# Gate columns of the memory branch projected among the memory attention's rounds, in a fused three-layer model kernel

## What is computed

```python
h = _rms(x, attn_norm_g)
mem_n = _rms(mem, mem_norm_g)                       # 256 memory rows
mk = _rms(_heads(mem_n @ w_kv[:, :MEM_W], 4), mem_k_norm_g)
mv = _heads(mem_n @ w_kv[:, MEM_W:], 4)
mq = _rms(_heads(proj("mem_q"), 4), mem_q_norm_g)   # proj(name) = h @ its columns of w_in
y_mem = _merge_heads(_mem_attention(mq, mk, mv))    # 4 heads of width 256
y_fox = ...   # attention with a forget gate: 16 heads, q and k normed per head
branches = jnp.stack([y_fox, y_lru, y_sb, y_mem], axis=2)
gates = jax.nn.sigmoid(proj("gates").reshape(b, s, 4, 1024) + b_gate)
mixed = jnp.sum(gates * jnp.einsum('bsnc,ncd->bsnd', branches, w_branch), axis=2)
x = x + mixed @ w_out
```

## Time and profile before

| what | value |
|---|---|
| runs, us | 4116.31 (median), 4113.97, 4118.38 |
| profiled execution, us | 4122.55, its span 4120.8 |
| TensorE busy | 3855.2 us, 94% of the span |
| VectorE, ScalarE, GpSimd busy | 1940.8, 1490.6, 381.7 us |
| memory attention's rounds | from 2573.8 to 2664.7 us of the span |
| memory branch | from 2664.7 to 2751.9 us |

### The profile page before, as it was taken

How to read it: one execution, slowest core, us unless ns; L and a number is a source line. 1 busy time by engine, 2 the same in 40 slices (tenths; PEclk the granted TensorE clock), 3 DMA queues, 4 the chain that set the end, 5 groups by cost and what they waited for, 6 DMA issues and landing times.

```text
span 4120.8 us, 48423 instructions
## 1 busy us (share of the span) xinstructions
PE 3855.2 (94%) x17196; PEld 3050.2 (74%) x17196; DVE 1940.8 (47%) x3222; ACT 1490.6 (36%) x2451; POOL 381.7 (9%) x332
## 2 busy tenths in 40 slices
PE   8999997799999999987899998899999999899999
PEld 6887664588888887665688886777777768677877
DVE  4433467654334423567554344335544444645652
ACT  3222343432223223333432234436535553533221
POOL 0100001101001101011011021101000000100110
PEclk9999998899999999987899999999999989999999
DMA  4333221033333333211133333131122113223332
GB/s 119 96 97 108 69 59 47 10 100 97 97 91 92 97 97 109 59 44 34 40 94 95 106 114 91 40 87 44 47 72 62 47 43 93 74 82 87 97 92 97
DMA packets 484448, 321.89 MB, mean 78 GB/s; under 512 B 10928, under 2 KB 464176, under 8 KB 483280
## 3 DMA queue, kind: packets, MB, share of 16 engines
q1 hardware_dynamic: 479616, 301.81, 25.2%
q0 software_dynamic: 3536, 16.13, 1.2%
q10 hardware_dynamic: 1152, 2.10, 0.1%
HBM read 310.82 MB, written 8.52 MB: 77 GB/s over the span
## 4 chain that ended last, share of the span: by engine, by line
PE 73%; DVE 8%; ACT 7%; issue 6%; DVEq 4%; POOLq 0%; DMA 0%; ACTq 0%; POOL 0%; SPq 0%
PE bank L234 21%; PE bank L236 20%; PE bank L235 20%; ACT w_hi L219 2%; DVE w_lo L226 1%; PE bank L1188 1%; PE bank L2152 1%; DVEq L2455 1%; PE bank L1199 1%; PE bank L1191 1%; PE bank L1190 1%; PE bank L1172 1%; PE bank L974 1%; DVEq L2469 1%; DVEq L1013 1%
## 5 line engine op out<-in xcount | busy, mean ns | idle before, releaser
L234 PE MATMUL bank<-h_hi,w_hi 128*128 128x512 f32 x3064 | 1230.0, 401 | 68.3 <-DVE h_lo L386 24.9
L226 DVE TENSOR_TENSOR w_lo<-w_raw,w_hi 128x1024 fp32r<-128x1024 f32 (+1 forms) x571 | 742.4, 1301 | 1070.8 <-ACT w_hi L219 1067.5
L236 PE MATMUL bank<-h_lo,w_hi 128*128 128x512 f32 x3128 | 1230.1, 393 | 0.0
L235 PE MATMUL bank<-h_hi,w_lo 128*128 128x512 f32 x3064 | 1204.7, 393 | 0.0
L219 ACT ACTIVATE w_hi<-w_raw 128x1024 fp32r<-128x1024 f32 (+1 forms) x571 | 591.5, 1038 | 620.0 <-DMA w_raw<-in_ffn_w_down 316.6
L234 PEld LDWEIGHTS bank<-h_hi,w_hi 128*128 128x128 f32 x3064 | 579.6, 189 | 236.8 <-issue 101.4
L236 PEld LDWEIGHTS bank<-h_lo,w_hi 128*128 128x128 f32 x3128 | 591.4, 189 | 131.3 <-issue 2.3
L235 PEld LDWEIGHTS bank<-h_hi,w_lo 128*128 128x128 f32 x3064 | 579.3, 189 | 114.5 <-issue 2.0
L234 PE MATMUL bank<-g_hi,w_hi 128*128 (+1 forms) x880 | 343.7, 391 | 3.7 <-DVE gu_ring L2471 3.7
L235 PE MATMUL bank<-g_hi,w_lo 128*128 (+1 forms) x880 | 343.4, 390 | 0.0
L236 PE MATMUL bank<-g_lo,w_hi 128*128 (+1 forms) x880 | 343.3, 390 | 0.0
(11 more groups left out here) (438 smaller groups left out, 4628.7 us busy)
## 6 DMA issues: line engine op xcount, KB each, us to landing
w_raw<-in_w_in SPq DMA_DIRECT2D x105, 512.0 KB, 3.8
w_raw<-in_ffn_w_gate SPq DMA_DIRECT2D x88, 512.0 KB, 3.8
w_raw<-in_ffn_w_up SPq DMA_DIRECT2D x88, 512.0 KB, 3.8
w_raw<-in_ffn_w_down SPq DMA_DIRECT2D x88, 512.0 KB, 3.5
w_raw<-in_w_mix SPq DMA_DIRECT2D x50, 512.0 KB, 3.9
w_raw<-in_w_up SPq DMA_DIRECT2D x44, 512.0 KB, 3.8
w_raw<-in_w_branch SPq DMA_DIRECT2D x32, 512.0 KB, 3.7
w_raw<-in_w_down SPq DMA_DIRECT2D x22, 512.0 KB, 3.2
```

The lines of the kernel that those rows point to most:

```text
L226: dve.tensor_tensor(WL[:, slot(c), 0:w], RAW[:, slot(c), 0:w], WH[:, slot(c), 0:w].bitcast(F32), ALU.subtract).then_inc(w_lo, 1)
L234: pe.matmul(bank, wh, xh, start=start, stop=False)
L235: pe.matmul(bank, wl, xh, start=False, stop=False)
L236: return pe.matmul(bank, wh, xl, start=False, stop=stop)
```

## The change

The eight gate units of the memory branch leave the branch and follow the six units of the first two head pairs, as eight `copy` items; the list of items laid among the memory attention's rounds grows from 6 to 14, and the parts on TensorE from 24 to 48, on ScalarE and VectorE from 8 to 16. Their raw sums are copied to the tiles of `X`. The branch becomes eight units of `w_branch`, written out instead of looped, over banks 0 to 3 in turn; ScalarE takes Sigmoid from the tiles of `X` into the same ring of two. Ahead of the first of these units TensorE waits for the low parts of all heads. Nothing else is moved; the number of units, matmuls and loads is what it was.

```diff
-U_BR["mem"] = _u; _u += 16
+U_GATES["mem"] = _u; _u += KT
+U_BR["mem"] = _u; _u += KT
...
+    def gate_items(name, unit0, dst, free):
+        out_ = [item(U_GATES[name] - unit0 + u, "copy", dst(u)) for u in range(KT)]
+        for u, x in enumerate(out_):
+            x["free"] = free(u)
+        return out_
...
-    PF1, PS1 = PF + 6, PF + 30
+    PF1, PS1 = PF + 14, PF + 38
...
+    fox_items0 += gate_items("mem", U_FOX0, lambda u: X[:, u, :], lambda u: (x_parked, LAYERS * 16 + 16))
...
+    def stored_branch_sp(sp, c, n):
+        for u in range(KT):
+            load_cols(sp, 0, c + u, A["w_branch_2"][n], u * P)
+
+    def stored_branch_act(act, c, b, n, gate):
+        act.preload_act_table(ACT.Sigmoid)
+        act.drain()
+        for u in range(KT):
+            hi(act, 0, c + u + AHEAD)
+            act.wait_ge(mx_done, b * KT + u + 1)
+            act.activation(SG[:, u % 2, :], gate(u), ACT.Sigmoid, bias=v2(W_BG + n * KT + u)).then_inc(sg_done, 1)
+
+    def stored_branch_dve(dve, c, b):
+        dve.drain()
+        for u in range(KT):
+            m = b * KT + u
+            lo(dve, 0, c + u + AHEAD)
+            dve.wait_ge(w_used, c + u + 5)
+            dve.wait_ge(sg_done, m + 3)
+            if b == 0:
+                dve.tensor_tensor(MIXED[:, u, :], SG[:, u % 2, :], B[u % 4][:, :], ALU.mult).then_inc(mx_done, 1)
...
+    def stored_branch_pe(pe, c, b, ready, bank_read):
+        bank_read(pe)
+        ready(pe)
+        for u in range(KT):
+            split_ready(pe, 0, c + u)
+            if u >= 4:
+                pe.wait_ge(mx_done, b * KT + (u - 4) + 3)
+            for k in range(KT):
+                last = products(pe, B[u % 4][:, :], c + u, slice(k * P, (k + 1) * P), YH[:, k, :], YL[:, k, :],
+                                k == 0, k == KT - 1)
+            last.then_inc(w_used, 1)
...
         pairs(U_FOX0, (FOXQ, FOXK, FOXV), 0, 2)
-        branch_sp(sp, C0 + U_BR["mem"], BRANCH["mem"])
+        for u in range(KT):
+            load_cols(sp, 0, C0 + U_GATES["mem"] + u, A["w_in_2"], GATE + BRANCH["mem"] * D + u * P)
+        stored_branch_sp(sp, C0 + U_BR["mem"], BRANCH["mem"])
...
-        branch_act(act, C0 + U_BR["mem"], 0, BRANCH["mem"])
+        stored_branch_act(act, C0 + U_BR["mem"], 0, BRANCH["mem"], lambda u: X[:, u, :])
...
-        branch_dve(dve, C0 + U_BR["mem"], 0, BRANCH["mem"])
+        stored_branch_dve(dve, C0 + U_BR["mem"], 0)
...
-        branch_pe(pe, C0 + U_BR["mem"], 0, lambda e: e.wait_ge(y_lo, YF + 2),
+        stored_branch_pe(pe, C0 + U_BR["mem"], 0, lambda e: e.wait_ge(y_lo, YF + 2),
                   lambda e: e.wait_ge(pt_done, SM + 16 + 2))
```

More of the change, by code:

```diff
@@ L70 @@
 U_MEMQ = U_FOXF + 1
-U_BR = {}
+U_BR, U_GATES = {}, {}
 _u = U_MEMQ + 8
 U_FOX0 = _u; _u += 6
-U_BR["mem"] = _u; _u += 16
+U_GATES["mem"] = _u; _u += KT
+U_BR["mem"] = _u; _u += KT
 U_FOX = _u; _u += 18
@@ L2068, in branch_dve @@
         dve.drain()
+    def stored_branch_sp(sp, c, n):
[17 more added lines that the diff above has]
+                dve.tensor_tensor(MIXED[:, u, :], SG[:, u % 2, :], B[u % 4][:, :], ALU.mult).then_inc(mx_done, 1)
+            else:
+                dve.tensor_tensor(GU[:, u % 2, :], SG[:, u % 2, :], B[u % 4][:, :], ALU.mult).then_inc(mx_done, 1)
+                dve.drain()
+                dve.tensor_tensor(MIXED[:, u, :], MIXED[:, u, :], GU[:, u % 2, :], ALU.add)
+        dve.drain()
+    def stored_branch_pe(pe, c, b, ready, bank_read):
[9 more added lines that the diff above has]
+            last.then_inc(w_used, 1)
     def branch_pe(pe, c, b, ready, bank_read):
```

## The result

| | kernel before | changed kernel |
|---|---|---|
| runs, us, median (lowest to highest), 14 each | 4113.85 (4106.36 to 4124.28) | 4125.22 (4120.69 to 4134.23) |
| ratio to before, 95% interval | | 1.003 [1.0022, 1.0038] |
| profiled execution, us, and its span | 4122.55, 4120.8 | 4128.55, 4126.6 |
| changed stretch, us | 183.69 | 190.43 |

The change makes the kernel 0.3% slower. The changed stretch is measured between two instructions that both kernels have: TensorE's first matmul of the woven units (2570.30 before, 2568.81 after, each behind the same wait of 1.50 us) and its first scores of the forgetting attention (2753.99 before, 2759.24 after). The lines of the file move by one: L234 of before is L235 of after, L1310 is L1311, L1362 is L1363.

A forecast was written before the change was run, and what follows sets the result against it. TensorE, busy 94% of the span, was taken as the bound, so only waits and clock counted: waits +5.2 and clock +3.7, about +9 us on 4116.3, gave 4125; own range 4120 to 4130, 8 in 10 within 4110 to 4133.

The forecast's parts named there:

- What bounds it: Whole kernel: TensorE busy 94%; moved work shortens a wait only if it lies behind the instruction starting the waiting chain.
- Boundaries: TensorE's waits for a finished head's banks in rounds 8, 12 and 16: 2.5, 2.70 and 2.70 us, before 5.32, 2.70 and 4.69.
- chain of round 12: Scores, row maximum, exponential, copy of turned probabilities, high part, low part, all in one round: TensorE idles 2.70 us.
- Bank 5: Seven rounds where one unit directly follows another: TensorE waits for ScalarE's copy out of the bank, 0.4 to 2.4 us each.
- The end: After the rounds, ahead of the new branch: the last head's high and low parts lie uncovered, 2.1 us of wait.
- Costs set at nothing: ScalarE's eight copies, Sigmoid from SBUF, loads, POOL's work and the written-out branch: no added time, the branch taking 43.6 us.
- Sum of waits: TensorE's waits in the rounds and at their end: 19.2 us new against 14.0 old, plus 5.2 us.
- Clock: TensorE's falls to half clock, about 2.5 us each: three boundaries keep theirs, one and a half more add 3.7 us.
- three doubtful waits: Waits at items 0 and 2 and at the end, between 1.29 us (no fall) and 2.70 us (fall); one and a half falls counted.
- Rival B: Same added waits, but the clock falls as often as before: +3 to +7 us, say 4121; chance 0.25.
- Rival C: Every wait above 2 us costs its own clock fall, six instead of three: +5 + 7.5 us, 4129; chance 0.15.
- Rival D: Faster: both roots leave the boundaries and fuller rounds keep the clock up at two of three: -8 us, 4108 at best; chance 0.10.

The follow-up runs named there:

- experiments 1 and 2: Heads taken out of their banks at the end of their last round: in the kernel before, 4102.08 us (0.9974); in the changed kernel, 4116.07 us (1.0001).
- experiment 4: Changed kernel with its last gate unit projected behind the rounds instead of in rounds 17 to 19: 4123.04 us, ratio 1.0027 to the kernel before.
- looped form: Changed kernel with the eight w_branch units in a loop of two turns of four: 4125.76 us (1.003); with all three edits as well, 4108.5 us (0.9987).
- all three edits: Changed kernel with heads taken early, last gate units (items 9, 11, 13) in bank 7, and last gate unit behind the rounds: 4111.03 us (0.9991).

## Why the prediction was right

The forecast was 4125, slower by 9; the runs gave 4125.22, slower by 11.4, in the way foretold. That the time itself was hit to 0.2 us is luck: the forecast started from 4116.3, the median of three runs, and the 14 runs have 4113.85; a start 2.5 us too high made up for a loss 2.4 us too small. Point by point:

- **What bounds it; moved work hides nothing unless it lies behind the start of a chain.** Right, and shown by experiments 1 and 2: at round 12 the wait was 2.69 us with parts of two units ahead of the scores and 2.70 with none, and the boundary waits went when the head was taken early. Round 8 is the other half: there the moved matmuls ran beside the table loads, and the exponential waited 2.71 us for the row maximum, not for its table.
- **Boundaries.** Round 8: 2.5 said, 2.69 measured. Round 12: 2.70 and 2.69. Round 16: 2.70 said, 1.78 measured. The mis-sized term: I carried the chain of round 12 over, but step 16 does not exist, so round 16 has no scores, row maximum or exponential; the chain starts at the turning. For the same reason the 4.69 us before had one table load in it and not two, as I said by round 8.
- **Bank 5.** 2.2 said and 2.15 measured for item 0; 2.4 and 2.42 for item 2; 0.4 and 0.39 for item 3; 1.6 and 1.53 for item 5; 0.85 and 0.78 three times. The v tiles went by the chain of round 8 replayed, not by the bare copies, and that was the right neighbour: ahead of both copies of a v tile ScalarE waits 2.01 us for VectorE's scaling of q.
- **The end.** 2.1 said (2666.91 - 2664.70 is 2.2) and 2.06 measured; shown by experiment 4.
- **Costs set at nothing.** Branch 43.60 us as said; the rounds 139 us (2574.39 to 2713.50), in the 134 to 145 given. Code written out: zero in the stretch (183.06 and 183.00 us against 183.10 and 183.69), perhaps a few us elsewhere, open.
- **Sum of waits.** 19.2 said, 18.1 measured; +5.2 and +4.1.
- **Clock.** +3.7 said; +2.7, +5.7 and +4.3 us of busy time in the three profiles, against the first of before. The number agrees, the parts do not. I had 4.5 falls at 2.5 us against three; measured were five, six and five falls behind the stretch's start against three and two. A fall of the kernel before cost about 2.5 us (14.9 us of work at half clock in three), one of the changed kernel about 1.7. That gives some 2.7 us on the mean, 0.8 in the first profile, and the edges of the waits, which I had not thought of, the 1.8 beside it. Of my three doubtful waits one (2.42) brought a fall in the first execution, two (2.15, 2.42) in the second, two (2.15 and the end) in the looped form; the wait of 1.53 us, which I had not counted, brought one in the first two. And the half clock that I placed after each long wait began inside two of them, where it costs nothing.
- **Rival B**, as many falls as before, is out: five or six against two or three.
- **Rival C.** Its +12.5 us is nearer to the runs' 11.4 than my 9, and the interval, +9.1 to +15.6, holds it and only just touches mine; the runs do not speak against it. The profiles do in part. Its rule, that each long wait pays the clock's change anew, is what the Trainium skill, "TensorE: Matmul & The Clock Gate", section "HAM oscillation — how this bites in real kernels", describes of a kernel whose bursts all start at the low clock. The three boundary waits paid each time in all three profiles of the changed kernel. The others did not: 2.15 us paid in one execution of this kernel and not in the other, and 1.53 us brought a fall where 2.06 us, in the same execution, did not.
- **Rival D** needed the boundary waits to lose their fall by themselves; in the changed kernel they kept it. (In the second profile of the kernel before the 2.69 us wait did lose it.)

## What to carry to other kernels

Before laying independent work among dependent rounds, follow each wait back to the instruction that starts its chain: work that comes ahead of that instruction delays the chain and fills nothing. Here taking a head out of its banks one round earlier was worth 11 us, and eight moved units cost as much. And units laid closer need the banks and rings for it; what shares one bank must not come back to back.

## What was not expected of the hardware

- The same program with the same waits spent 172.37 and 175.40 us of busy time in one stretch: the clock's answer to a wait of 2.15 us differs between executions. With all three edits the four waits brought two falls, and the same four waits in the looped form none (165.87 and 162.88 us busy). Waits repeat to 0.02 us, their clock can be forecast only as a chance.
- The mean granted clock says little by itself: in the first profiles it rose from 0.94 to 0.95 in the stretch while the clock's cost grew, since before the change 5.5 of the 23.3 us at half clock lay in waits, after it 0.4 of 19.8.
- The unchanged 2570 us ahead of the change vary by 19 us between executions, with mean clock 0.95 to 0.96. A difference of a few us between two kernels has to be read from a stretch, not from two spans, and its busy time from more than one profile.
